# Stick-breaking attention on one core: the transposes of the weights of two neighbouring key tiles issued together, in every second slot

## The chip, the core and the metric

The kernel runs on one core of a Trainium2 chip. The metric is the device time of one launch in microseconds (us). The engines are named as the profile names them: PE (TensorE; its weight loads are PEld), DVE (VectorE), ACT (ScalarE), POOL (GpSimd) and SP, which issues the DMAs.

## The reference, cut to what matters

One decoder block over 2048 tokens of width 1024: an input projection, a gated MLP branch (A), a stick-breaking attention branch (B, 8 heads of width 128), the two branches projected, gated and merged, an output projection, a residual and a norm. The change touches branch B only:

```
logits = einsum('bthd,bshd->bhts', q_blk, k) * scale          # per block of 128 queries
log_beta = log_sigmoid(logits)
log_one_minus = where(causal, log_beta - logits, 0)           # causal: key < query
suffix = cumsum(log_one_minus, reverse) - log_one_minus
weights = where(causal, exp(log_beta + suffix), 0)
y_b = einsum('bhts,bshd->bthd', weights, v)
```

In words: a query's weight on a key is sigmoid(logit) times the product of (1 - sigmoid) over all keys between the two.

## The kernel before

The program has three stages: the input projection (to about 1479 us of the span), the attention (1479 to 2204 us) and the merge with the output projection. All float32 products are made of two halves, `hi` and `lo`, and three matmuls (hi hi, lo hi, hi lo).

**The unit of work of the attention** is a *piece*: 128 queries against up to 512 keys (a *unit* is 512 queries against 512 keys, so four pieces; a diagonal unit has pieces 128, 256, 384 and 512 keys wide). 8 heads of 10 units give 320 pieces. A unit gives also four *turns*, one for each tile of 128 keys. The work is laid out in *slots*, one piece a slot, by `Pieces.in_slots`. Each engine walks the same list of events in the same order and does its own part of each:

- `Z n`, piece n. PE: three matmuls for the logits (lines 1636 to 1638) into one of three PSUM banks. ACT: two sigmoids (1521, 1522). DVE: a running product along the keys, the *scan* (1576, on the diagonal tile also 1566). POOL: the two multiplied into the weights (1488).
- `B m`, turn m. PE: up to four 128x128 transposes of weights (1661) into one of three PSUM banks `t_ps`. ACT: the hi copy (1542) to `wT_hi`. DVE: the lo rest (1596) to `wT_lo`. A turn needs all four pieces of its unit.
- `P m`, turn m. PE: three matmuls with V (1672 to 1674), added up in the single bank `y_ps`. Its first matmul waits for the lo rest of turn m: `pe.wait_ge(lo_copied, max(w.step_of["B", m], ...) + 1)` (1669).
- `Y i`, 32 times: DVE multiplies the finished `y_ps` with a gate (1604). It waits for the last `P` of its 512 queries, and DVE takes a `Y` or `G` ahead of all else of its slot (line 1211).
- `F f`, 256 of them: three matmuls of branch A's output projection (1684 to 1686) that fill PE, spread over slots 22 to 300. `G`, 32 times: DVE's gating of eight of them (1609), behind the last `F`.
- `K` and `V`: loads of the next head's q, k, v, and of branch A's tiles, that are split into hi and lo (ACT 1510 and POOL 1476; for `V` PE transposes at 1650, ACT 1529, DVE 1586).

Before the change slot s holds `Z s`, its `K` or `V`, `B s-6`, its `F` and `G`, `P s-8` and its `Y`. The constants are `LAG = 6` and `BEHIND = 2`. ACT, DVE and POOL work strictly in the order of this list, and so does PE.

Of the kernel before, what the change touches and what calls it, by code (L numbers as in the profile page):

```python
# [1180 lines left out]
LAG = 6  # L1181
# [6 lines left out]
class Pieces:  # L1188
# [26 lines left out]
    def in_slots(self):  # L1215

        at = {}

        def put(slot, event):
            at.setdefault(slot, []).append(event)  # L1220

        start = {(h, sup, g): QT * n for n, (h, sup, g) in enumerate(self.units)}
        wanted = []
        for h in range(HEADS):
            first = start[h, NSUP - 1, NSUP - 1]
            for sup in reversed(range(NSUP)):

                need = start[h, NSUP - 1, sup]
                free_k = start[h - 1, sup, sup] + QT if h else -1
                free_q = start[h - 1, sup, 0] + QT if h else -1  # L1230
                free_v = free_k + LAG + BEHIND + 1 if h else -1
                wanted.append((max(free_k, need - 5, -1), ("k", h, sup)))
                wanted.append((max(free_v, need + 2), ("v", h, sup)))
                wanted.append((max(free_q, start[h, sup, sup] - 6, -1), ("q", h, sup)))
        n_slots = len(self.pieces) + LAG + BEHIND
        fills, n_fills = {}, HEADS * QT * KT

        slot_of = [F_FIRST + f // KT * (F_END - F_FIRST) // (HEADS * QT) + f % KT for f in range(n_fills)]
        for f in range(n_fills):
            fills.setdefault(slot_of[f], []).append(f)  # L1240

        for h in range(HEADS):
            for j in range(KT):
                wanted.append((slot_of[(QT * h - 1) * KT + j] + 1 if h else FIRST if j < N_EARLY_A else 3 * (j - N_EARLY_A) + 6, ("a", h, j)))
        for half in range(2):
            for r in range(QT):
                for part in range(2):
                    free = slot_of[(HEADS * QT // 2 - QT + r) * KT + KT - 1] + 1 if half else F_FIRST - 8 + 9 * r + 4 * part
                    wanted.append((free, ("w", half * QT + r, part)))


        for c in range(KT):
            for part in range(2):
                if c < QT:
                    free = slot_of[((HEADS - 1) * QT + c) * KT + KT - 1] + 1
                else:
                    free = slot_of[-1] + 1 + (2 * (c - QT) + part) * 2
                wanted.append((free, ("o", c, part)))
        wanted.sort(key=lambda w: (w[0], w[1][1], -w[1][2], "kqvawo".index(w[1][0])))
        self.items = [item for _, item in wanted]  # L1260
        for slot, item in wanted:
            put(slot, ("V" if item[0] == "v" else "K", item))
        slots = [at.pop(-1, []) + at.pop(FIRST, [])]
        for slot in range(n_slots):
            order = []
            slots.append(order)
            if slot < len(self.pieces):
                order.append(("Z", slot))
            order += at.pop(slot, [])
            if 0 <= slot - LAG < len(self.turns):  # L1270
                order.append(("B", slot - LAG))
            for f in fills.get(slot, []):
                order.append(("F", f))
                if f % KT == KT - 1:
                    order.append(("G", f // KT))
            m = slot - LAG - BEHIND
            if 0 <= m < len(self.turns):
                order.append(("P", m))
                h, sup, g, kt = self.turns[m]
                if kt == QT - 1 and g == 0:  # L1280
                    order.append(("Y", h * NSUP + NSUP - 1 - sup))
        return slots
# [1105 lines left out]
```

## Time and profile before

| | before |
|---|---|
| time, 3 runs (us) | 2553.91, 2553.76, 2552.14; median 2553.76 |
| span of the profiled execution | 2553.1 us |
| PE busy | 2487.6 us (97%) |
| DVE, ACT, POOL busy | 1599.8, 1301.8, 1259.0 us |
| attention, first to last instruction of PE | about 1479 to 2204 us |

No time of its own is given for the profiled execution beside its span; the span is 0.7 us under the median of the runs. A busy PE means that matmul records cover the time; matmuls overlap, and the end of each is modelled, so a short wait of PE is partly hidden in such a row and is better read from the distance between starts.

### The profile page before, as it was taken

The page shows a single profiled execution, that of the slowest core. Times are in us where ns is not written, and L with a number is a line of the kernel's source. Part 1 is how long each engine was busy: PE and PEld are TensorE (multiplying, and loading weights), DVE is VectorE, ACT ScalarE, POOL GpSimd, SP SyncE. Part 2 cuts the span into 40 slices and gives each one's busy share as a digit, 9 for nine tenths or more (in the row PEclk, how much of TensorE's full clock was granted, in tenths as well). Part 3 has the DMA queues.
Part 4 walks back from the last instruction along what each step waited for, and adds up shares of the span by engine and source line. Part 5 has one row for each costly group of instructions (what it writes and reads, how often), then busy time and mean ns, then how long its engine had stood idle before and what let it go on. Part 6 is the DMA issues. An engine that isn't in the chain of part 4 may idle for free. (4 is left out here: it accounts for less than half of the span.)

```text
span 2553.1 us, 34995 instructions
## 1 busy us (share of the span) xinstructions
PE 2487.6 (97%) x11925; PEld 2065.2 (81%) x11925; DVE 1599.8 (63%) x2091; ACT 1301.8 (51%) x2372; POOL 1259.0 (49%) x1127
## 2 busy tenths in 40 slices
PE   7999999999989999999999999999999999999898
PEld 5788888888878888888888878888888888778787
DVE  7545555555575555555555588788788888532676
ACT  6664333344354543444444377677777777411343
POOL 2544332332344544344343367667766777633464
PEclk9999999999999999999999999999999999999999
DMA  3333333333325344445544344334433434577542
GB/s 124 99 99 116 123 103 105 121 103 111 115 70 149 107 141 140 136 141 144 152 142 131 123 142 124 96 112 137 118 101 114 124 108 125 197 259 280 198 151 113
DMA packets 280632, 338.01 MB, mean 132 GB/s; under 512 B 16408, under 2 KB 181280, under 8 KB 280480
## 3 DMA queue, kind: packets, MB, share of 16 engines
q1 hardware_dynamic: 276880, 329.58, 41.6%
q10 hardware_dynamic: 3600, 6.56, 0.7%
q8 instruction: 77, 1.26, 0.2%
q14 instruction: 75, 0.61, 0.1%
HBM read 222.83 MB, written 113.25 MB: 132 GB/s over the span
## 5 line engine op out<-in xcount | busy, mean ns | idle before, releaser
L1028 PE MATMUL in_bank<-carried_hi,in_w_hi 128*128 128x512 f32 x1988 | 783.3, 394 | 14.0 <-DVE carried_last L822 9.9
L1031 PE MATMUL in_bank<-carried_hi,in_w_lo 128*128 128x512 f32 x1988 | 775.2, 390 | 0.0
L1030 PE MATMUL in_bank<-carried_lo,in_w_hi 128*128 128x512 f32 x1988 | 775.0, 390 | 0.0
L1028 PEld LDWEIGHTS in_bank<-carried_hi,in_w_hi 128*128 128x128 f32 x1988 | 373.9, 188 | 93.5 <-DVE carried_last L822 11.7
L1031 PEld LDWEIGHTS in_bank<-carried_hi,in_w_lo 128*128 128x128 f32 x1988 | 373.7, 188 | 78.7
L1030 PEld LDWEIGHTS in_bank<-carried_lo,in_w_hi 128*128 128x128 f32 x1988 | 374.1, 188 | 74.9
L548 ACT ACTIVATE in_w_hi<-in_sums 128x512 fp32r<-128x512 f32 x284 | 178.5, 630 | 470.0 <-PE in_bank L1031 317.3
L1576 DVE TENSOR_TENSOR_SCAN att_rest<-att_z_ps,att_rest 128x512 f32<-128x512 f32 (+3 forms) x288 | 317.5, 1103 | 45.9 <-ACT att_z_ps L1522 26.8
L417 POOL TENSOR_TENSOR in_sums<-carried_stage 128x512 f32<-128x512 f32 x71 | 97.1, 1368 | 439.0 <-DMA carried_stage<-in_w_in 417.8
L753 DVE TENSOR_TENSOR in_w_lo<-in_sums,in_w_hi 128x512 fp32r<-128x512 f32 x284 | 274.1, 966 | 55.2 <-ACT in_w_hi L548 47.7
L822 DVE TENSOR_TENSOR carried_last<-in_bank,in_o 128x512 f32<-128x512 f32 x71 | 49.1, 692 | 303.2 <-PE in_bank L1031 56.5
L753 DVE TENSOR_TENSOR in_w_lo<-carried_stage,in_w_hi 128x512 fp32r<-128x512 f32 x213 | 207.2, 973 | 24.3 <-ACT in_w_hi L548 22.2
L548 ACT ACTIVATE in_w_hi<-carried_stage 128x512 fp32r<-128x512 f32 x213 | 133.7, 628 | 143.0 <-PE in_bank L1031 73.4
L1488 POOL TENSOR_TENSOR carried_wide<-carried_wide,att_rest 128x512 f32<-128x512 f32 (+3 forms) x160 | 151.0, 946 | 91.1 <-DVE att_rest L1576 86.5
L1476 POOL TENSOR_TENSOR carried_lo<-carried_wide,carried_hi 128x512 fp32r<-128x512 f32 x152 | 195.2, 1292 | 0.0
L1596 DVE TENSOR_TENSOR att_wT_lo<-att_t_ps,att_wT_hi 128x512 fp32r<-128x512 f32 (+1 forms) x320 | 188.6, 590 | 4.6 <-ACT att_wT_hi L1542 4.4
L1542 ACT ACTIVATE att_wT_hi<-att_t_ps 128x512 fp32r<-128x512 f32 (+1 forms) x320 | 170.5, 533 | 4.8 <-PE att_t_ps L1661 4.6
L1522 ACT ACTIVATE att_z_ps<-att_z_ps 128x512 f32<-128x512 f32 (+2 forms) x320 | 171.2, 535 | 0.0
L1521 ACT ACTIVATE carried_wide<-att_z_ps 128x512 f32<-128x512 f32 (+3 forms) x160 | 85.4, 534 | 81.5 <-PE att_z_ps L1638 81.1
L1672 PE MATMUL att_y_ps<-att_wT_hi,carried_hi 128*128 128x512 f32 (+1 forms) x320 | 120.8, 377 | 3.9 <-DVE carried_wide L1604 2.1
L1636 PE MATMUL att_z_ps<-carried_hi 128*128 128x512 f32 (+2 forms) x320 | 117.9, 368 | 4.5 <-PEq L46 3.7
L1684 PE MATMUL att_f_ps<-carried_hi 128*128 128x512 f32 x256 | 122.0, 477 | 0.0
(219 smaller groups left out, 4787.8 us busy)
## 6 DMA issues: line engine op xcount, KB each, us to landing
carried_stage<-in_w_in SPq DMA_DIRECT2D x144, 512.0 KB, 4.7
carried_wide<-ya_T SPq DMA_DIRECT2D x64, 256.0 KB, 3.4
uz_T<-in_o SPq DMA_DIRECT2D x32, 256.0 KB, 4.7
carried_wide<-va_T SPq DMA_DIRECT2D x16, 512.0 KB, 5.7
carried_wide<-uz_T SPq DMA_DIRECT2D x16, 512.0 KB, 6.3
ya_T<-in_x_sb SPq DMA_DIRECT2D x16, 512.0 KB, 4.9
carried_wide<-k_T SPq DMA_DIRECT2D x32, 256.0 KB, 3.2
carried_wide<-q_T SPq DMA_DIRECT2D x32, 256.0 KB, 3.4
```

What stands on the lines that cost most here:

```text
L548: act.activation(w_hi[:, i], left[i], ACT.Copy).then_inc(w_hi_done[i], 1)
L753: dve.tensor_tensor(w_lo[:, i], left[i], w_hi[:, i].bitcast(F32), ALU.subtract)\
L1028: pe.matmul(bank[:, :], hi, a_hi[:, i, k], start=opens and k == 0, stop=False, skip_group_check=True)
L1030: pe.matmul(bank[:, :], hi, a_lo[:, i, k], start=False, stop=False, skip_group_check=True)
L1031: mm = pe.matmul(bank[:, :], lo, a_hi[:, i, k], start=False, stop=k == HALF_K - 1, skip_group_check=True)
L1476: pool.tensor_tensor(lo, src, hi.bitcast(F32), ALU.subtract).then_inc(split_done, 1)
L1488: pool.tensor_tensor(a, a, rest[r][:, left + 1:left + width + 1], ALU.mult).then_inc(weighted, 1)
L1522: act.activation(src, src, ACT.Sigmoid, scale=-SCALE).then_inc(rest_done, 1)
L1542: act.activation(wT_hi[m % W_BUFS][:, c0:], bank_of(step)[:, c0:], ACT.Copy).then_inc(hi_copied, 1)
L1576: dve.tensor_tensor_scan(out=row[:, left:left + width][:, ::-1], data0=z_ps[n % Z_BANKS][:, 0:width][:, ::-1], data1=row[:, S:S + 1].to_br ...
L1596: dve.tensor_tensor(wT_lo[b][:, c0:], bank_of(step)[:, c0:], wT_hi[b][:, c0:].bitcast(F32), ALU.subtract).then_inc(lo_copied, 1)
L1684: pe.matmul(f_ps[:, :], wo_hi[:, j, cols], ya_hi[:, j], start=j == 0, stop=False)
```

## The change

A turn with an even number is now issued one slot later, ahead of the odd turn behind it: odd slots hold two `B`, even slots none. `P m` stays in slot m + 8, and everything else stays in its slot.

```diff
-            if 0 <= slot - LAG < len(self.turns):
-                order.append(("B", slot - LAG))
+            if 0 < slot - LAG < len(self.turns) and (slot - LAG) % 2:
+                order += [("B", slot - LAG - 1), ("B", slot - LAG)]
```

The same list drives PE, ACT and DVE, so the copies of the even turns move too. On PE, in slots 103 and 104 of the third head, before (`att_z_ps` logits, `att_t_ps` transposes, `att_f_ps` filling, `att_y_ps` product with V; first the last matmul of `Z 103`, at the end `P 96`):

```order
 L1638 MATMUL att_z_ps<-carried_hi,carried_lo 128x512
 L1661 MATMUL att_t_ps<-carried_ident,att_slot 128x128 x2
 L1661 MATMUL att_t_ps<-carried_ident,carried_last 128x128
 L1684 MATMUL att_f_ps<-carried_hi 128x512
...
 L1674 MATMUL att_y_ps<-att_wT_hi,carried_lo 128x512
 L1636 MATMUL att_z_ps<-carried_hi 128x512
...
 L1661 MATMUL att_t_ps<-carried_ident,att_slot 128x128
 L1661 MATMUL att_t_ps<-carried_ident,carried_last 128x128
 L1684 MATMUL att_f_ps<-carried_hi 128x512
...
 L1672 MATMUL att_y_ps<-att_wT_hi,carried_hi 128x512
```

And now:

```order
 L1638 MATMUL att_z_ps<-carried_hi,carried_lo 128x512
 L1661 MATMUL att_t_ps<-carried_ident,carried_wide 128x128
 L1661 MATMUL att_t_ps<-carried_ident,att_slot 128x128 x2
 L1661 MATMUL att_t_ps<-carried_ident,carried_last 128x128
 L1661 MATMUL att_t_ps<-carried_ident,att_slot 128x128 x2
 L1661 MATMUL att_t_ps<-carried_ident,carried_last 128x128
 L1684 MATMUL att_f_ps<-carried_hi 128x512
...
 L1674 MATMUL att_y_ps<-att_wT_hi,carried_lo 128x512
 L1636 MATMUL att_z_ps<-carried_hi 128x512
...
 L1684 MATMUL att_f_ps<-carried_hi 128x512
...
 L1672 MATMUL att_y_ps<-att_wT_hi,carried_hi 128x512
```

The four transposes of turn 96 came in from slot 102, and the two of turn 98 left slot 104. On DVE at the same place, before (`att_rest` the scans, `att_wT_lo` the lo rests, `carried_wide<-att_y_ps` the `Y` of slot 103):

```order
 L1596 TENSOR_TENSOR att_wT_lo<-att_t_ps,att_wT_hi 128x512
 L1604 TENSOR_TENSOR carried_wide<-att_y_ps,carried_wide 128x512
 L1576 SCALAR_TENSOR_TENSOR att_rest<-att_z_ps,att_rest 128x512
 L1596 TENSOR_TENSOR att_wT_lo<-att_t_ps,att_wT_hi 128x384
 L1576 SCALAR_TENSOR_TENSOR att_rest<-att_z_ps,att_rest 128x512
 L1596 TENSOR_TENSOR att_wT_lo<-att_t_ps,att_wT_hi 128x256
```

And now:

```order
 L1604 TENSOR_TENSOR carried_wide<-att_y_ps,carried_wide 128x512
 L1576 SCALAR_TENSOR_TENSOR att_rest<-att_z_ps,att_rest 128x512
 L1596 TENSOR_TENSOR att_wT_lo<-att_t_ps,att_wT_hi 128x512
 L1596 TENSOR_TENSOR att_wT_lo<-att_t_ps,att_wT_hi 128x384
 L1576 SCALAR_TENSOR_TENSOR att_rest<-att_z_ps,att_rest 128x512 x2
```

The lo rest of turn 96 (512 wide) stood ahead of this `Y` and of the scan of slot 103, and stands behind both now.

## Rows read from the trace of the kernel before

**Rows 1.** The page: busy time, share of the span, instructions.

```profile
PE 2487.6 (97%) x11925; PEld 2065.2 (81%) x11925; DVE 1599.8 (63%) x2091; ACT 1301.8 (51%) x2372; POOL 1259.0 (49%) x1127
```

**Rows 2.** Stretches: length, busy time by engine, granted clock of PE, DMA share, GB/s.

```profile
1480.00:1484.00 4.00, 3.06 (x12) 2.46 (x12) 2.68 (x5) 2.22 (x7) 1.92 (x6) 0.50 0.88 210
1522.00:2160.00 638.00, 632.65 (x3488) 534.04 (x3487) 515.94 (x727) 469.51 (x994) 455.96 (x522) 1.00 0.39 115
1672.00:1676.00 4.00, 1.67 (x12) 1.23 (x11) 3.13 (x4) 2.95 (x8) 4.00 (x4) 1.00 0.61 174
```

**Rows 3.** Who waited for whom, 1485 to 2205: us, times, longest.

```profile
PE att_t_ps L1661 <- POOL carried_wide L1488: 2.3, 3, 1.1
PEld att_y_ps L1672 <- DVE att_wT_lo L1596: 5.1, 13, 0.9
```

**Rows 4.** Timeline of slots 103 and 104, with a Y: start, duration.

```profile
1705.84 0.39 PE L1638 MATMUL att_z_ps<-carried_hi,carried_lo 128*128 128x512 f32 x1
1706.08 0.38 PE L1661 MATMUL att_t_ps<-carried_ident,att_slot 128*128 128x128 f32 x2
1706.29 0.27 PE L1661 MATMUL att_t_ps<-carried_ident,carried_last 128*128 128x128 f32 x1
...
1707.56 0.39 PE L1674 MATMUL att_y_ps<-att_wT_hi,carried_lo 128*128 128x512 f32 x1
...
1707.99 0.69 DVE L1604 TENSOR_TENSOR carried_wide<-att_y_ps,carried_wide 128x512 f32<-128x512 f32 x1 [1.16 <-PE att_y_ps L1674]
...
1708.60 1.27 DVE L1576 TENSOR_TENSOR_SCAN att_rest<-att_z_ps,att_rest 128x512 f32<-128x512 f32 x1
...
1709.40 0.39 PE L1672 MATMUL att_y_ps<-att_wT_hi,carried_hi 128*128 128x512 f32 x1
```

**Rows 5.** Timeline of slots 131 and 132, with two F.

```profile
1768.84 0.39 PE L1638 MATMUL att_z_ps<-carried_hi,carried_lo 128*128 128x512 f32 x1
...
1769.76 0.59 ACT L1522 ACTIVATE att_z_ps<-att_z_ps 128x512 f32<-128x512 f32 x1
...
1770.48 1.28 DVE L1576 TENSOR_TENSOR_SCAN att_rest<-att_z_ps,att_rest 128x512 f32<-128x512 f32 x1 [0.15 <-ACT att_z_ps L1522]
...
1771.68 0.67 DVE L1596 TENSOR_TENSOR att_wT_lo<-att_t_ps,att_wT_hi 128x512 fp32r<-128x512 f32 x1
...
1772.36 0.40 PE L1672 MATMUL att_y_ps<-att_wT_hi,carried_hi 128*128 128x512 f32 x1
...
1772.83 0.40 PE L1674 MATMUL att_y_ps<-att_wT_hi,carried_lo 128*128 128x512 f32 x1
```

**Rows 6.** Timeline of slots 107 and 108, with a G in slot 107.

```profile
1715.93 0.40 PE L1686 MATMUL att_f_ps<-carried_hi,carried_lo 128*128 128x512 f32 x1
...
1716.37 0.69 DVE L1609 TENSOR_TENSOR carried_stage<-att_f_ps,carried_stage 128x512 f32<-128x512 f32 x1 [0.26 <-PE att_f_ps L1686]
...
1716.98 1.27 DVE L1576 TENSOR_TENSOR_SCAN att_rest<-att_z_ps,att_rest 128x512 f32<-128x512 f32 x1
...
1717.94 0.39 PE L1672 MATMUL att_y_ps<-att_wT_hi,carried_hi 128*128 128x512 f32 x1
1718.17 0.67 DVE L1596 TENSOR_TENSOR att_wT_lo<-att_t_ps,att_wT_hi 128x512 fp32r<-128x512 f32 x1
```

**Rows 7.** Timeline: a product with V that waited for its lo rest.

```profile
2161.14 0.67 DVE L1596 TENSOR_TENSOR att_wT_lo<-att_t_ps,att_wT_hi 128x512 fp32r<-128x512 f32 x1
...
2161.86 0.50 PE L1672 MATMUL att_y_ps<-att_wT_hi,carried_hi 128*128 128x512 f32 x1 [0.16 <-DVE att_wT_lo L1596]
...
2162.20 0.39 PE L1673 MATMUL att_y_ps<-att_wT_lo,carried_hi 128*128 128x512 f32 x1
```

**Rows 8.** Timeline, PE: first matmuls of turns 0, 14, 292 and 316.

```profile
1492.54 0.51 PE L1672 MATMUL att_y_ps<-att_wT_hi,carried_hi 128*128 128x512 f32 x1 [0.16 <-DVE att_wT_lo L1596]
...
1519.14 0.40 PE L1672 MATMUL att_y_ps<-att_wT_hi,carried_hi 128*128 128x512 f32 x1
...
2157.67 0.48 PE L1672 MATMUL att_y_ps<-att_wT_hi,carried_hi 128*128 128x512 f32 x1
...
2200.91 0.47 PE L1672 MATMUL att_y_ps<-att_wT_hi,carried_hi 128*128 128x512 f32 x1 [0.76 <-DVE carried_wide L1604]
```

## The prediction

> **What bounds the kernel now.** I read the page first: PE is busy 97% of the span [rows 1], so nothing but PE's work and PE's waits can move the time. The table of stretches says the same of the attention: from 1522 to 2160 us PE is busy 632.65 of 638.00 us at the full clock (1.00, that is 2.4 GHz), while DVE has 122 us to spare [rows 2]. The list of waits then says how thin PE's waits are: all waits of products for DVE's lo rests are 5.1 us in 13 waits, those of transposes for POOL's weights 2.3 us [rows 3]. So the change can win little. Last the timelines, since what it can lose is hidden in distances between starts: how long before PE comes to `P` is its lo rest ready?
>
> **Units.** Three matmuls 512 wide take PE 0.70 us: from a transpose at 1706.29 to the sixth matmul behind it at 1707.56 are 1.27 us, one transpose (0.11, from the pairs at 1706.08 to 1706.29) and five matmuls of 0.23 [rows 4]. A full turn is four transposes, 0.44 us. The number of instructions on each engine does not change, and the rows show no cost of going from matmul to transpose and back, since 0.11 + 5 x 0.232 is all of that distance. Fewer such changes therefore save nothing, and I cost the grouping itself at zero. From below, 320 borders less at the 5 ns that these readings leave open would be 1.6 us saved.
>
> **What moves.** Turn 2k goes from slot 2k+6 to slot 2k+7, but `P 2k` stays in slot 2k+8. On DVE its lo rest now stands behind the scan of slot 2k+7. So a new chain runs from PE's own logits back to PE: last matmul of `Z 2k+7` to the second sigmoid 0.92 (1768.84 to 1769.76), to the scan 0.72 (1770.48), to the lo rest 1.20 (1771.68), the lo rest 0.67 [rows 5], and to the product 0.05 (2161.14 + 0.67 to 2161.86) [rows 7]. That is 3.56 us. A product that had to wait also pays 0.10 more: its second matmul starts 0.34 behind its first, not 0.23 [rows 7]. Against the 3.56 stands what PE does between: the rest of that matmul 0.23, now eight transposes 0.88, `F` 0.70, `P 2k-1` 0.70, `Z 2k+8` 0.70, `F` 0.70, together 3.91. Before, the lo rest of an even turn was a slot ahead of this, some 2 us clear. Now it is clear by 0.35 at best. Behind the stalled `P 2k` on PE stands `Z 2k+9`, which starts the next chain, so a stall isn't given back: the next scan cannot start before those logits.
>
> **The sum, by kinds of pairs (slots 2k+7 and 2k+8).** I did the same subtraction, end of the odd slot's scan plus lo rest against the start of `P 2k`, for every pair of the trace, and give one example of each kind.
>
> 1. *Pairs with a Y, 30.* All 32 `Y` are in odd slots (two behind the last logits). DVE takes it first, and it needs `P 2k-1`. In slot 103: third matmul of P 95 at 1707.56, Y 0.43 later, scan 0.61 after that [rows 4], lo rest 1.19 later [rows 6] and 0.67 long, product 0.05: 2.95, and 0.10 for the blocked start, 3.05. PE has the rest of P 0.23, Z 0.70 and F 0.70 in that time, 1.63. The stall is 1.42 us. It is 0.70 more where the even slot has no F (5 of 30), 0.36 more where the next logits are 128 wide (8), 0.25 more where the scan is a diagonal one in two parts (7): (5 x 0.70 + 8 x 0.36 + 7 x 0.25) / 30 = 0.27 more, 1.70 on average. 30 x 1.70 = 51 us.
> 2. *Pairs with a G in the odd slot and no Y, 13.* G stands 0.44 behind the last F matmul (1715.93 to 1716.37), scan 0.61, lo rest 1.19 and 0.67, product 0.05 and 0.10: 3.06 [rows 6, 7]. PE has 0.23 + 0.70 + 0.70 + 0.70 = 2.33 with all full, and 1.59 in the example, where P and Z are 128 wide: a stall of 0.73 to 1.47; over all 13, 1.15. 15 us.
> 3. *Plain pairs in the filled slots, 98.* Half have slack. In the example P 123 is 128 wide, so PE is at P 124 after 3.52 [rows 5] against 3.66: 0.14 of stall. Four pairs of each head's 20 fall short in this way. Turns 4 and 8 have one 128-wide product or logits between (PE's 3.91 less 0.37, and 0.15 short). Turn 20 has both (0.5 short), turn 32 both and a diagonal scan besides (0.8). That is 1.6 a head, over seven heads 11 us. Pairs with one F (8) are 0.45 short, 4 us; a few hundredths on other pairs with a diagonal scan make 2 us more. 17 us.
> 4. *Pairs without F, 15 at the start and the end.* The cycle becomes the chain, 3.66 + 0.70 (P) + 0.46 (Z up to its last matmul) = 4.82. Now it is 3.80 at the start (1492.54 to 1519.14, seven pairs) and 3.60 at the end (2157.67 to 2200.91, twelve) [rows 8], some shorter for diagonal pieces, and so would the chain be. 1.0 to 1.2 each: 17 us.
>
> Together 100 us. **To take off:** PE stalls that exist now and would be swallowed. PE's idle time from 1522 to 2160 is 5.3 us by its row [rows 2], about 7 by the distances between starts. A later `B 4u` also finds POOL's weights ready. I take 7 off: **+93 us**. The sum is made against the profiled span, 2553.1 + 93 = 2646 us, and the median of the runs lies 0.7 above that span: 2647 us. The bounds: kinds 1 and 2 alone, less 7, are +59; all of it with nothing taken off, and 0.15 more (the 0.10 and 0.05 of a blocked start once again) on each of the 110 or so pairs that stall, are +117.
>
> **The clock.** After the 2.3 us wait of PE around 1673 us the granted clock stays 1.00, although PE was busy only 1.67 of 4.00 us there; at the entry to the attention, behind a longer thin stretch, it was 0.50 (1.2 GHz) [rows 2]. The new stalls are 0.1 to 2.2 us, so I charge nothing. The Trainium skill (TensorE: Matmul & The Clock Gate, Part 4: PE-mode transpose) holds that transposes do not count as PE work for the clock gate, which speaks against putting eight of them beside a stall. This trace has transposes throughout the attention at 1.00, and by that rule the outcome would be rival 3 below.
>
> **The rivals.**
> 1. *Forecast,* +93, chance 0.72.
> 2. *Only Y and G pairs stall,* +59, 2613 us. It needs the plain chain to be shorter than I read it, and the cycle at the start and the end to stay as now. Against it: even now products wait for lo rests 13 times [rows 3], with a whole slot more of time, so the wait is real wherever the rest is late. Chance 0.14.
> 3. *Forecast plus a lower clock* where PE is thinnest, the 15 pairs of kind 4. Their PE work is 3.66 us at full clock (two Z, two P, eight transposes) and 7.3 at half, 2.5 more than the chain: 15 x 2.5 = 38 us, 2685 us. For it the 0.50 at the entry, against it the 1.00 around 1673. Chance 0.08.
> 4. *The other side, faster.* One mechanism: `B 4u` waits in PE's order for the four weighted pieces, and PE waits 2.3 us and more for POOL there [rows 3]; one slot later these waits go. It decides only if the lo rests of even turns come in time after all, that is if the chain of 3.66 stays under PE's 3.91 also in Y pairs, where I count 3.05 against 1.63. Price: all of the 7 us of stalls, 2547 us. Chance 0.04.
> 5. *No change that shows:* DVE lets the lo rest pass in time and nothing waited for POOL. Chance 0.02.
>
> **How the numbers follow.** A measurement of this kernel tells about 0.2% (5 us) from no change. Faster 0.04, same 0.02, slower 0.94. The range takes in rival 2 and the upper bound, 2610 to 2671; rival 3 and the small cases are left out.
>
> **What would show each step.** Right: the stages before 1479 us and after the attention as long as now; the attention about 93 us longer with the same count and mean of every matmul; products at L1672 that wait for DVE's lo rest L1596 some 100 times for about 90 us, those behind a Y 1.4 to 2.1 us each; DVE and ACT idle for the logits more than now. Waits of L1661 for POOL gone. Wrong: stalls behind Y under 1 us (then DVE does not keep the order that I read), waits at the transposes for free banks in place of those at the products, or a granted clock under 1.00 inside the attention.

## The result, and the profile after

| | before | after |
|---|---|---|
| median (us) | 2553.76, 5 runs (2551.12 to 2556.38) | 2651.31, 5 runs (2644.93 to 2652.50) |
| ratio | | 1.0375, 95% interval 1.0363 to 1.0387: slower by 96 us |
| span of the profiled execution | 2553.1 | 2650.8 (its own time 2652.5) |
| projection, up to PE's first matmul of the attention | 1479.1 | 1475.8 |
| attention, up to PE's first matmul of the merge | 725.5 | 823.6 |
| merge | 348.5 | 351.4 |

The forecast was 2647 us in 2610 to 2671. (The 96 us are 3.75% of the median before; the two medians themselves and the two spans differ by 97.6 and 97.7.) All of the difference lies in the attention, +98.1 us; the other two stages differ by 3 us in opposite directions. The page of the kernel after answers to [rows 1]; its second row is the group of the waiting products (mean ns, idle time before, what ended it):

```profile
PE 2519.8 (95%) x11925; PEld 2077.6 (78%) x11925; DVE 1607.5 (61%) x2091; ACT 1299.2 (49%) x2372; POOL 1266.4 (48%) x1127
...
L1672 PE MATMUL att_y_ps<-att_wT_hi,carried_hi 128*128 128x512 f32 (+1 forms) x320 | 130.3, 407 | 80.4 <-DVE att_wT_lo L1596 80.4
```

Every engine has the same number of instructions, and DVE, ACT and POOL are as long busy as before, to 8 us. PE's row rises by 32 us without more work. One matmul's row is 0.39 long and the next starts 0.23 behind it, so most rows overlap by 0.16; in front of a wait they don't, and the product that waited is drawn 0.50 long and not 0.40. How much of the 32 us is this and how much the lower clock of the last section was not separated. The list of waits from 1485 to 2299 us answers to [rows 3]:

```profile
PEld att_y_ps L1672 <- DVE att_wT_lo L1596: 119.5, 106, 2.8
...
PE att_y_ps L1672 <- DVE att_wT_lo L1596: 80.4, 76, 2.3
```

Waits of PE for DVE's lo rests went from 5.1 us in 13 to 119.5 us in 106 at the weight load. (The weight load's wait counts from the end of the last load, so it is longer than the time lost.) Waits of the transposes (L1661) for POOL are no longer in the list. Now the three timelines of the forecast again. Slots 103 and 104, with a Y, answer to [rows 4]:

```profile
1731.88 0.39 PE L1638 MATMUL att_z_ps<-carried_hi,carried_lo 128*128 128x512 f32 x1
...
1734.03 0.39 PE L1674 MATMUL att_y_ps<-att_wT_hi,carried_lo 128*128 128x512 f32 x1
1734.46 0.69 DVE L1604 TENSOR_TENSOR carried_wide<-att_y_ps,carried_wide 128x512 f32<-128x512 f32 x1 [1.74 <-PE att_y_ps L1674]
...
1735.07 1.27 DVE L1576 TENSOR_TENSOR_SCAN att_rest<-att_z_ps,att_rest 128x512 f32<-128x512 f32 x1
...
1736.26 1.13 DVE L1596 TENSOR_TENSOR att_wT_lo<-att_t_ps,att_wT_hi 128x512 fp32r<-128x512 f32 x2
...
1736.98 0.50 PE L1672 MATMUL att_y_ps<-att_wT_hi,carried_hi 128*128 128x512 f32 x1 [1.16 <-DVE att_wT_lo L1596]
...
1737.32 0.39 PE L1673 MATMUL att_y_ps<-att_wT_lo,carried_hi 128*128 128x512 f32 x1
```

Read it down: product 95 ends, Y, scan, then the two lo rests in one row, and product 96 starts 0.05 behind the first of them. From the third matmul of product 95 to product 96 are 2.95 us, the figure of the forecast. Slots 131 and 132, plain with two F, answer to [rows 5]:

```profile
1805.48 0.40 PE L1638 MATMUL att_z_ps<-carried_hi,carried_lo 128*128 128x512 f32 x1
...
1806.40 0.59 ACT L1522 ACTIVATE att_z_ps<-att_z_ps 128x512 f32<-128x512 f32 x1
...
1807.13 1.28 DVE L1576 TENSOR_TENSOR_SCAN att_rest<-att_z_ps,att_rest 128x512 f32<-128x512 f32 x1 [0.32 <-ACT att_z_ps L1522]
...
1808.33 1.26 DVE L1596 TENSOR_TENSOR att_wT_lo<-att_t_ps,att_wT_hi 128x512 fp32r<-128x512 f32 x2
...
1809.05 0.50 PE L1672 MATMUL att_y_ps<-att_wT_hi,carried_hi 128*128 128x512 f32 x1
```

The chain from the logits to the product is 3.57 us (forecast 3.56). And slots 107 and 108, with a G, answer to [rows 6]:

```profile
1744.05 0.39 PE L1686 MATMUL att_f_ps<-carried_hi,carried_lo 128*128 128x512 f32 x1
...
1744.48 0.69 DVE L1609 TENSOR_TENSOR carried_stage<-att_f_ps,carried_stage 128x512 f32<-128x512 f32 x1 [1.05 <-PE att_f_ps L1686]
...
1745.09 1.27 DVE L1576 TENSOR_TENSOR_SCAN att_rest<-att_z_ps,att_rest 128x512 f32<-128x512 f32 x1
...
1746.28 1.26 DVE L1596 TENSOR_TENSOR att_wT_lo<-att_t_ps,att_wT_hi 128x512 fp32r<-128x512 f32 x2
...
1747.00 0.50 PE L1672 MATMUL att_y_ps<-att_wT_hi,carried_hi 128*128 128x512 f32 x1 [0.82 <-DVE att_wT_lo L1596]
```

The terms of the sum can be read from both traces as well: the distance from the third logits matmul (L1638) of one odd slot to that of the next is the length of a pair, and the pairs sort into the four kinds. ("Without F" are the 15 pairs whose odd slot lies before 22 or from 300 on.) One thing has to be taken off: the change also moves transposes from one pair to the next, and where the turn that comes in has four and the one that leaves has two (as in the order shown above) a pair grows by 0.22 us of plain work. That is counted from the order at 0.11 us a transpose.

| kind | pairs | before | after | more | moved work | net | forecast |
|---|---|---|---|---|---|---|---|
| Y in the odd slot | 30 | 131.4 | 188.4 | 57.0 | 6.6 | 50.4 | 51 |
| G in the odd slot, no Y | 13 | 56.1 | 67.4 | 11.3 | -1.1 | 12.4 | 15 |
| plain, filled | 98 | 458.6 | 468.9 | 10.4 | -5.1 | 15.4 | 17 |
| without F | 15 | 57.0 | 73.5 | 16.5 | -0.4 | 16.9 | 17 |
| old stalls swallowed | | | | | | in the above | -7 |
| sum | 156 | 703.1 | 798.3 | 95.2 | 0 | 95.2 | 93 |

Not every pair stalls. Read as the distance from the matmul before to the product, over the usual 0.23, PE waits more than 0.1 us in front of the even turn's product in all 30 Y pairs (1.28 to 2.31 us each), in 12 of the 13 G pairs, in 26 of the 98 plain ones and in 10 of the 15 without F: 78 of 156.

Behind slot 319 the last turns take 3.5 us more (10.3 and 13.8 us to the last matmul), which the forecast had left out.

### The profile page after: what moved, and what is told of

It reads as the page before. It is cut to its first block and busy times, and to the rows that moved or that the text cites. A ratio compares the mean times of both kernels' runs of the same rounds, so it can differ in the third digit from the quotient of the medians.

```text
span 2650.8 us, 34995 instructions
## 1 busy us (share of the span) xinstructions
PE 2519.8 (95%) x11925; PEld 2077.6 (78%) x11925; DVE 1607.5 (61%) x2091; ACT 1299.2 (49%) x2372; POOL 1266.4 (48%) x1127
## 5 line engine op out<-in xcount | busy, mean ns | idle before, releaser
L753 DVE TENSOR_TENSOR in_w_lo<-carried_stage,in_w_hi 128x512 fp32r<-128x512 f32 x213 | 214.2, 1006 | 23.4 <-ACT in_w_hi L548 21.2
L1672 PE MATMUL att_y_ps<-att_wT_hi,carried_hi 128*128 128x512 f32 (+1 forms) x320 | 130.3, 407 | 80.4 <-DVE att_wT_lo L1596 80.4
L1596 DVE TENSOR_TENSOR att_wT_lo<-att_t_ps,att_wT_hi 128x512 fp32r<-128x512 f32 (+1 forms) x320 | 176.9, 593 | 2.6 <-ACT att_wT_hi L1542 2.6
L1672 PEld LDWEIGHTS att_y_ps<-att_wT_hi,carried_hi 128*128 128x128 f32 x320 | 60.9, 190 | 127.4 <-DVE att_wT_lo L1596 119.5
L1542 ACT ACTIVATE att_wT_hi<-att_t_ps 128x512 fp32r<-128x512 f32 (+1 forms) x320 | 152.0, 530 | 6.6 <-PE att_t_ps L1661 6.5
```

The source lines that it names most:

```text
L753: dve.tensor_tensor(w_lo[:, i], left[i], w_hi[:, i].bitcast(F32), ALU.subtract)\
L1542: act.activation(wT_hi[m % W_BUFS][:, c0:], bank_of(step)[:, c0:], ACT.Copy).then_inc(hi_copied, 1)
L1596: dve.tensor_tensor(wT_lo[b][:, c0:], bank_of(step)[:, c0:], wT_hi[b][:, c0:].bitcast(F32), ALU.subtract).then_inc(lo_copied, 1)
L1672: pe.matmul(y_ps[:, c0:], v_hi[:, ks], wT_hi[b][:, c0:], start=first, stop=False)
```

## The experiments

Theory 1 is that of the forecast: the loss is the place of the even turn's lo rest in DVE's order, behind the next odd slot's scan, Y and G, on a chain that starts with PE's logits of that slot. Theory 2: the loss is made on PE, by eight transposes in a row. The other rivals are the granted clock and ACT's order. All ratios are to the kernel before on the same chip.

**The two sides of the change apart.** The program makes both lists of events and gives one engine the other list.

```diff
-            for e, i in vector_events:
+            for e, i in w.paired_vector_events[w.n_early:]:      # DVE alone
```

> PE, ACT and POOL walk the list of the kernel before; DVE alone walks the list of the change, so that each even turn's lo rest stands behind the scan (and the Y or G) of the next odd slot, while every transpose stays where it was. Theory 1 (the loss is the lo rest's place on DVE): nearly all of the loss is there, 75 to 100 us over before, with PE waiting at L1672 for L1596 some 90 times. Theory 2 (the loss is PE's: eight transposes in a row, and what they do to banks and clock): no change within 5 us.

Measured: ratio 1.0368 (1.0351 to 1.0385), 94 us over before.

```diff
-            for e, i in events:
+            for e, i in w.paired_events[w.n_early:]:             # PE alone
                 if e == "Z":
                     logits(i)
```

> PE alone walks the list of the change, eight transposes in a row in odd slots; ACT, DVE and POOL keep the list of before, with an even turn's copies ahead of the odd slot's sigmoids and scan. Theory 1: the lo rest is early, but the sigmoids of odd slots start about 1 us later, since the hi copy of the even turn stands ahead of them and waits for its transposes; that is hidden in filled slots and costs 5 to 10 us where there is no F: 0 to 15 us over before. Theory 2: 75 to 100 us over before.

Measured: 1.0017 (1.0007 to 1.0026), 4 us. So with no transpose moved, DVE's order alone costs as much as the change, to 2 us, and the grouped transposes with DVE and ACT as before cost 4. Of these 4, 2.6 lie in the last turns behind slot 319 and less than 1 in all the pairs together. The equal totals are partly chance, for the kinds differ: with DVE alone Y pairs are 42.6 us over before (57.0 in the change, 50.4 net), G pairs 9.7, plain ones 24.5 (10.4, 15.4 net) and those without F 16.3. The waits of the run with DVE alone (lines are shifted by 8) show a difference of place: a fifth of them are at the transposes (L1669), which wait for a free bank, and the rest at the products:

```profile
PEld att_y_ps L1680 <- DVE att_wT_lo L1604: 100.5, 100, 2.5
PEld att_t_ps L1669 <- DVE att_wT_lo L1604: 18.5, 25, 1.4
```

Theory 2 falls as the cause.

**The largest term.** The even turn keeps its own slot where the odd slot behind it holds a Y.

```diff
+                if m % 2:
+                    order += [("B", m - 1), ("B", m)] if together(slot) else [("B", m)]
+                elif not together(slot + 1):
+                    order.append(("B", m))
...
+        def together(slot):
+            return not any(s + LAG + BEHIND == slot for s, (_, _, g, kt) in enumerate(self.turns) if g == 0 and kt == QT - 1)
```

> The change, but the two turns are not put together where the odd slot holds a Y (32 of 160 pairs), for which the even turn stays in its own slot. Theory 1, kind 1 of the sum: the 50 to 57 us of these pairs go and the rest stays, 38 to 45 us over before. If the loss were spread evenly over the pairs (theory 2, or a cost of each group), only a fifth of it would go, and it would stay 75 to 80 us over before.

Measured: 1.0202 (1.0185 to 1.0219), 52 us over before: 44 went, not 50 to 57. That is far from a fifth of the loss, so a Y pair is special, but the expectation was too high. It took the 57 us of raw length for a stall, of which 6.6 are moved work. Net of that, the Y pairs are 1.6 us over before in this run, so 48.8 of their 50.4 went. The plain pairs are at 18.3 (15.4 in the change) and those with G at 14.8 (12.4), 5 us that went back, while those without F are at 13.3 (16.9), 4 us less.

**The unfilled stretches.** The same edit with `return F_FIRST <= slot < F_END`.

> The change only in slots 22 to 299; in the slots without filling matmuls at the start and the end each turn stays in its own slot. Kind 4 of the sum and the two Y of that stretch go: 17 to 22 us less than the change, 74 to 79 us over before, and the half-clock stretches at 1503 to 1523 and behind 2260 us are not there. If these stretches of low clock added a cost of their own, 10 us more than that goes.

Measured: 1.0262 (1.0246 to 1.0278), 67 us over before, 29 less than the change. By net lengths the 15 pairs gave back 18.5 us (from 16.9 over before to 1.6 under), the Y pairs 6.3, of which two lie in this stretch, and the last turns behind slot 319 their 3.5: together 28 of the 29 us. The expectation had left out the last of these. No further 10 us went, so the low clock there had no price of its own that shows, although from 2228 us to the end of the attention the granted clock is 1.00 in this run, too. The first 40 us of both runs, the change and then this one (length, busy PE, PEld, DVE, ACT and POOL, granted clock):

```profile
1486.00:1526.00 40.00, 32.66 (x159) 26.88 (x158) 29.69 (x39) 28.32 (x60) 27.78 (x30) 0.87 0.27 73
```

```profile
1486.00:1526.00 40.00, 37.96 (x204) 30.40 (x203) 36.42 (x47) 34.11 (x73) 34.17 (x35) 1.00 0.31 88
```

**More time for the product.** The change with each product one slot later.

```diff
-BEHIND = 2
+BEHIND = 3
```

> The change with BEHIND = 3: each product with V one slot later (the loads of v, which count from it, too), so that an even turn's lo rest has a slot more, as before the change. Theory 1: the waits at L1672 go, 5 us under to 8 us over before. Theory 2: the eight transposes are as they were, 75 us and more over before. If the lower granted clock were the cause and not a result of the stalls, it would stay too.

Measured: 0.9976 (0.9966 to 0.9986), 6 us under before: the loss is gone with the eight transposes still in a row. Its control is the kernel before with the same edit.

> The kernel before (turns one by one) with BEHIND = 3, beside the run of the change with BEHIND = 3 that was 6 us under before. If that gain comes from the later products (and loads) alone, this is as fast: 3 to 8 us under before. If it comes from the grouping (transposes that no longer wait for POOL's weights), this stays within 2 us of before.

Measured: 0.9982 (0.9973 to 0.9991), 5 us under before. Both were run again side by side:

> The change with BEHIND = 3 again, now beside the kernel before with BEHIND = 3 on one chip, to tell them apart: 4 to 8 us under before.

Measured: 0.9982 (0.9974 to 0.9991).

> The kernel before with BEHIND = 3 again, on the same chip: 3 to 6 us under before. If the grouping adds anything of its own where the products have time, it is 1 to 3 us slower than the run with pairs; that is at the edge of what five rounds can tell.

Measured: 0.9989 (0.9980 to 0.9998). The two can't be told apart by these times: both intervals hold 0.9980 to 0.9991. The gain is in the main the later products'. The run with pairs has the lower median both times, by 1 to 2 us, and in the profiled executions its attention took 721.0 and 721.1 us, that of single turns 723.2 and 723.7 (725.5 before). So some 2 us for the grouping are likely, and not shown beyond that. PE's waits show what it does there. In both runs with pairs, 1485 to 2197 us:

```profile
PE att_t_ps L1661 <- DVE att_wT_lo L1596: 5.7, 8, 1.5
PE att_y_ps L1672 <- DVE carried_wide L1604: 3.4, 3, 1.7
```

In the run with single turns of the second comparison:

```profile
PE att_y_ps L1672 <- DVE carried_wide L1604: 3.6, 3, 1.5
PE att_t_ps L1661 <- POOL carried_last L1488: 3.3, 2, 1.8
PE att_t_ps L1661 <- POOL carried_wide L1488: 2.3, 4, 0.7
```

The grouping does take away the waits for POOL's weights, as rival 4 said, and PE's rows show more waits for a free bank of `t_ps` in their place (5.7 us in 8, against 0.8 in one): two turns in one slot take two of the three banks at once. At the weight loads, though, such waits are as long with single turns (9.9 us in 9) as with pairs (9.0 in 13), so that these waits eat up the gain is not shown.

**The lo rest first.** DVE takes the even turn's lo rest ahead of the odd slot's Y, G and scan.

```diff
-        ... for e in sorted(slot, key=lambda e: e[0] not in "YG")]
+        ... for e in sorted(slot, key=lambda e: (e[0] not in "YG") + 1 if e[0] != "B" or e[1] % 2 else 0)]
```

> The change, but DVE takes the even turn's lo rest first in its odd slot, ahead of Y, G and the scan; PE and ACT keep the pairs. Theory 1: the chain to the even product is about 2.7 us and not 3.56, the stalls of all kinds go, 0 to 10 us over before. A theory in which ACT's order counts (its hi copy of the even turn stands behind the odd slot's two sigmoids) would leave half of the loss, 40 us.

Measured: 1.0133 (1.0118 to 1.0149), 34 us over before. The first expectation did not hold; the second, 40 us if ACT's order counts, came nearer. By net lengths, plain, G and unfilled pairs are 3 to 5 us over before each, and 22 us are left in the Y pairs. There PE now waits for the Y itself, and DVE for ACT (rows of the list of waits):

```profile
DVE att_wT_lo L1596 <- ACT att_wT_hi L1542: 150.7, 152, 2.7
...
PE att_y_ps L1672 <- DVE carried_wide L1604: 19.1, 23, 1.8
```

The lo rest waits for its hi copy, and that stands on ACT behind two sigmoids and, in most Y slots, behind a split K. DVE is in order, so Y waits with it, and the scan behind Y. The test is to take the hi copies ahead of the K on ACT, all else as in this run.

```diff
+        self.scalar_events = [e for slot in in_slots for e in sorted(slot, key=lambda e: e[0] == "K")]
...
-            for e, i in events:
+            for e, i in w.scalar_events[w.n_early:]:             # ACT
```

> As the run with the lo rest first on DVE (35 us over before, 28 of them in pairs with a Y), with one more step: ACT takes the hi copies of a slot ahead of its splits K of the next head, which stand 0.5 us each behind the sigmoids in most odd slots with a Y. If Y waits on DVE behind the even turn's lo rest, and that for a hi copy behind a K, then 10 to 20 us of the 35 go. If Y pairs are slow for another reason, nothing goes.

Measured: 1.0055 (1.0040 to 1.0070), 14 us over before; 20 of the 34 went, 14 of them in the Y pairs. The same two rows (lines shifted by 1):

```profile
DVE att_wT_lo L1597 <- ACT att_wT_hi L1543: 121.2, 150, 1.8
...
PE att_y_ps L1673 <- DVE carried_wide L1605: 8.6, 9, 1.7
```

**The first link.** PE and DVE as in the change, ACT as before, which makes the sigmoids of odd slots later.

> PE and DVE walk the list of the change, ACT that of before: its hi copy of the even turn stands ahead of the odd slot's sigmoids and waits for transposes that now come behind that slot's logits, so these sigmoids start about 1.0 us later. If the chain is logits, sigmoids, scan, lo rest, product, it is 4.6 us and not 3.56 in pairs without Y or G, 0.7 us or more over PE's 3.91 in about 98 of them and 1.0 more in 15 unfilled ones: 150 to 180 us over before. If what counts is only when the hi copy is there, it is earlier now and the loss is at most that of the change, 97 us.

Measured: 1.0646 (1.0631 to 1.0662), 165 us over before. Behind the logits of a plain pair's odd slot, the hi copy starts after 0.87 us in the median (1.44 in the change), the second sigmoid after 1.84 (0.92), the lo rest after 3.77 (2.85). The copy is earlier and the loss 70 us larger, so it is the chain through the sigmoids and the scan that counts. The run with PE alone had its sigmoids as late (1.84) and lost almost nothing, since its lo rest did not stand behind the scan and started after 1.50. Products waited for lo rests 154 times (lines shifted by 8):

```profile
PEld att_y_ps L1680 <- DVE att_wT_lo L1604: 195.7, 154, 3.3
```

By raw lengths, plain pairs went from 10.4 to 66.2 us over before and unfilled ones from 16.5 to 29.5, while Y and G pairs stayed (55.7 and 11.6, where the change has 57.0 and 11.3): in these it is Y or G, not the sigmoids, that the scan comes behind.

**The other parity.** An odd turn waits for the next even one, in the even slot.

```diff
+            if 0 <= slot - LAG <= len(self.turns) and (slot - LAG) % 2 == 0:
+                order += [("B", m) for m in (slot - LAG - 1, slot - LAG) if 0 <= m < len(self.turns)]
```

> The pairs one slot over: an odd turn is held back to the even slot behind it, together with the next even turn. All Y are in odd slots, so the kind that cost 51 to 57 us is gone; kinds 2 to 4 remain with 16 G in even slots, and new is that the sigmoids of every second even slot wait for the held-back turn's transposes (ACT's slot is reused), 0.4 us each: 40 to 70 us over before. If a Y were not special, it would be as slow as the change.

Measured: 1.0264 (1.0248 to 1.0280), 67 us over before, 29 us better than the change and within what was expected. Where the Y stand is not all that differs, since 16 of the 32 G now lie in the slots with two turns, and the Y pairs did not become free. With pairs counted from one even slot's logits to the next, net of moved work, the 30 with a Y are 19.0 us over before, the 12 with a G in the even slot and no Y 13.9, the 13 with a G in the odd slot 1.8, the 86 plain ones 20.2 and the 15 without F 13.1. What the later sigmoids have in this was not separated.

## Why the prediction was right

The likeliest rival came true in its mechanism, its place and its size, 96 us where 93 were forecast. That the total is so near is partly luck, as the terms below show.

- *PE is the bound, and only its waits matter:* right. The attention grew by 98 us while the work of every engine stayed.
- *Grouping costs nothing on PE:* right, by the run with PE alone (4 us) and by the change with later products (6 us under before). What the expectation of that run held for likely, 5 to 10 us in pairs without F for ACT's later sigmoids, did not come: these pairs are 0.3 us over before, and 2.6 of the 4 us lie behind slot 319, for a reason that was not looked into.
- *The new chain of 3.56 us and 0.05 to the product:* right, 3.57 in the pair shown, and its first link by the run with ACT's list of before, its last by the run with DVE alone.
- *Kind 1, Y pairs, 51 us:* 50.4 net, and the run without them gave 48.8 back. Each stall behind a Y was to be 1.4 to 2.1 us; they are 1.28 to 2.31.
- *Kinds 2 and 3, 15 and 17:* 12.4 and 15.4. The G pairs were the term most off, 0.95 a pair and not 1.15.
- *Kind 4, 17:* 16.9. The 3.5 us behind slot 319 were forgotten, and stand against the 5 us by which the four terms were too high together (95.2 of 100).
- *The 7 us taken off for swallowed stalls:* they cannot be told from these differences. The four terms without them are 5 us over the measured 95.2, so the 7 us may have made up for terms that were too high.
- *A stall isn't given back:* right to about 5 us in 49, by the run without the Y pairs.
- *The clock, charged nothing:* the premise was wrong, the price nearly right. A granted clock under 1.00 inside the attention was one of the signs named as wrong, and it came. The last section has its rows.
- *Rival 4's mechanism,* the waits for POOL, was real: the waits went. In the change their gain of a few us is lost in the stalls, and where the products had time some 2 us of it are likely, as told above.

## What to carry to other kernels

When a step is moved later in a list that several engines share, look at each engine's own queue for what it now stands behind, not at the step's length: here a copy of 0.67 us that passed behind a scan of 1.3 us turned a slack (2.1 us in the median of the Y pairs, 2.35 in the plain ones, 0.75 in those without F) into a stall at every second product of an even turn. Measure the slack, from the end of the producer to the start of its consumer, in the trace of before, and sort it by what else stands in the slot; the sum over these kinds gave the loss to 3%, and each kind to 3 us. If a producer is batched, try moving its consumer by as much in the same edit: here one slot more for the products took away all of the 96 us.

## What the runs showed of the hardware that was not expected

The granted clock fell inside the attention, where the forecast had charged nothing. Before, it is 1.00 from 1486 to 1526 us; in the change it is 0.98 over the stage, and between 1492 and 1502 us, and after it, the level of 0.5 (1.2 GHz) shows in part of each stretch, while PE was still busy 8 of 10 us in the records (before, then twice the change):

```profile
1486.00:1526.00 40.00, 38.25 (x207) 30.50 (x206) 38.13 (x49) 36.12 (x77) 34.05 (x36) 1.00 0.34 101
```

```profile
1492.00:1502.00 10.00, 8.21 (x42) 6.85 (x41) 7.31 (x9) 7.73 (x17) 7.89 (x8) 0.84 0.46 133
1503.00:1506.00 3.00, 3.00 (x14) 2.55 (x13) 2.46 (x3) 1.47 (x4) 2.33 (x2) 0.69 0.25 70
```

The grouped transposes by themselves do not do it, and the stalls by themselves do. The run with PE alone has the same eight in a row with few stalls and 1.00 over 1486 to 2205 us; the run with DVE alone groups none, has the stalls, and falls to 0.96 in its first 40 us (in this order):

```profile
1486.00:2205.00 719.00, 703.48 (x3879) 596.11 (x3877) 596.84 (x828) 529.85 (x1134) 522.33 (x593) 1.00 0.37 111
```

```profile
1486.00:1526.00 40.00, 30.53 (x162) 24.06 (x162) 29.75 (x38) 29.04 (x60) 28.79 (x30) 0.96 0.29 86
```

By this the premise of rival 3 was half right: repeated stalls did lower the clock, and more transposes together, without stalls, did not. Both together lowered it further, to 0.87 in the same 40 us, with about as many matmuls there as with DVE alone (159 against 162). Whether that is the transposes beside the stalls or the other places of the stalls, no run separates. The Trainium skill (TensorE: Matmul & The Clock Gate, Part 4: PE-mode transpose) says that transposes do not count as PE work for the clock gate. The run with PE alone shows no effect of that, at 1.00; beside stalls, where 0.87 stands against 0.96, it stays open.

The price is small. From 1486 to 2299 us the granted clock is 0.98 in the change and 0.99 in the run with DVE alone, 1% of 813 us or about 8 us of full-speed time between them, and the two times differ by 2 us. Against a clock of 1.00, 0.98 is 2% of 813 us, some 16 us, and that is about the most that it can have cost. The likely reason why less shows is that the chain and not PE's work sets the time where PE is thin. No run changed the clock alone, so the price is bounded and not measured, and what it was is contained in the net terms of the table.
